# Eight gathers in a row: four U rows then four V rows, in place of U and V in turn

## What is computed

```
eidx = ...                                   # 16 experts per token and head
u = u_tab[eidx]; v = v_tab[eidx]             # rows of 1024 float32
h = gelu(einsum('td,thkd->thk', xk, u))
coef = gate * h
out = einsum('thk,thkd->td', coef, v)
```

## Time and profile before

| | us |
|---|---|
| median of 3 runs | 3058.2 (3057.4 to 3060.53) |
| the profiled execution's own time | 3057.73 |
| its span | 3055.9 |

### The profile page before, as it was taken

How to read it: one execution, slowest core, us unless ns; L and a number is a source line. 1 busy time by engine, 2 the same in 40 slices (tenths; PEclk the granted TensorE clock), 3 DMA queues, 4 the chain that set the end, 5 groups by cost and what they waited for, 6 DMA issues and landing times.

```text
span 3055.9 us, 27644 instructions
## 1 busy us (share of the span) xinstructions
PE 1719.7 (56%) x7829; PEld 779.9 (26%) x7829; DVE 2176.4 (71%) x5291; ACT 917.3 (30%) x3111; POOL 2056.4 (67%) x2169
## 2 busy tenths in 40 slices
PE   8875556777768576666433333355535444335435
PEld 8852223444334233333100000111101111001102
DVE  8787678877776678888766666666677777666553
ACT  2334324333333323322321123333223332123302
POOL 2146667666676776767577777777777777777774
PEclk9987878888889788888665556677757777557668
DMA  6379999999999999999999999999999999999997
GB/s 179 109 270 404 399 400 398 393 391 341 378 386 390 407 404 404 406 398 402 401 401 409 406 405 409 407 407 408 406 409 402 406 409 403 409 401 408 409 409 276
DMA packets 369741, 1165.94 MB, mean 382 GB/s; under 512 B 35433, under 2 KB 95417, under 8 KB 369589
## 3 DMA queue, kind: packets, MB, share of 16 engines
q0 software_dynamic: 304128, 1107.43, 91.9%
q1 hardware_dynamic: 64928, 55.92, 5.7%
q10 hardware_dynamic: 533, 0.83, 0.1%
HBM read 1158.88 MB, written 5.15 MB: 381 GB/s over the span
## 4 chain that ended last, share of the span: by engine, by line
DMA 36%; DVE 25%; POOL 17%; issue 9%; PE 6%; ACT 1%; POOLq 0%; SPq 0%; DVEq 0%; ACTq 0%
DMA ex_u_row<-in_u_tab_dram,ex_eidx 19%; DVE ex_u_row L1991 11%; POOL ex_v_row L1256 9%; POOL ex_u_row L1256 8%; DMA ex_v_row<-in_v_tab_dram,ex_v_idx 8%; DMA ex_u_row<-in_u_tab_dram,m_first_idx 6%; PE ex_acc L1883 3%; DMA ex_u_row<-in_u_tab_dram,ex_few_idx 2%; PE ex_turn L1724 1%; DMA m_wq<-in_w_in_dram 1%; DVE ex_same L1927 1%; DVE ex_same L1929 1%; DVE ex_idx L1930 1%; DVE ex_weight L1985 1%; DVE ex_best_at L1923 1%
## 5 line engine op out<-in xcount | busy, mean ns | idle before, releaser
L1991 DVE CUSTOM_DVE_ANT_0 ex_u_row<-ex_u_row,ex_xn 128x1024 f32<-128x1024 f32 x1056 | 1267.2, 1216 | 717.8 <-DMA ex_u_row<-in_u_tab_dram,ex_eidx 523.5
L1883 PE MATMUL ex_acc<-ex_v_row,ex_weight 128*32 128x512 f32 x4096 | 775.7, 896 | 1168.3 <-DMA ex_v_row<-in_v_tab_dram,ex_v_idx 1158.1
L1256 POOL DMA_INDIRECT ex_v_row<-in_v_tab_dram,ex_v_idx x1024 | 979.7, 957 | 485.7 <-issue 273.5
L1256 POOL DMA_INDIRECT ex_u_row<-in_u_tab_dram,ex_eidx x768 | 737.6, 960 | 242.3 <-issue 176.2
L1883 PEld LDWEIGHTS ex_acc<-ex_v_row,ex_weight 128*32 128x32 f32 x4096 | 155.1, 141 | 1657.7 <-issue 1645.4
L1256 POOL DMA_INDIRECT ex_u_row<-in_u_tab_dram,m_first_idx x256 | 245.7, 960 | 150.3 <-DVEq L2153 72.5
L1483 ACT ACTIVATE ex_hact<-ex_hdot 128x16 f32<-128x16 f32 x66 | 14.3, 216 | 777.7 <-DVE ex_hdot L1991 777.5
L1593 PE MATMUL ex_q<-m_mix,m_wq 128*128 128x384 f32 (+1 forms) x704 | 226.5, 476 | 0.0
L1320 ACT COPY ex_spread_coef<-ex_coef 32x4 f32<-32x4 f32 x1024 | 195.8, 191 | 53.7 <-DVE ex_coef L1976 41.7
L1593 PEld LDWEIGHTS ex_q<-m_mix,m_wq 128*128 128x128 f32 x704 | 135.8, 199 | 103.6 <-issue 42.8
L1309 ACT COPY ex_v_idx<-ex_eidx 32x4 uint32<-32x4 uint32 x768 | 146.0, 190 | 8.3
(11 more groups left out here) (422 smaller groups left out, 2254.7 us busy)
## 6 DMA issues: line engine op xcount, KB each, us to landing
ex_v_row<-in_v_tab_dram,ex_v_idx POOLq DMA_INDIRECT x1024
m_wq<-in_w_q_dram SPq DMA_DIRECT2D x14, 1024.0 KB, 16.5
ex_u_row<-in_u_tab_dram,ex_eidx POOLq DMA_INDIRECT x768, 8.9
fr_w<-in_w_in_dram SPq DMA_DIRECT2D x12, 512.0 KB, 4.7
ex_u_row<-in_u_tab_dram,m_first_idx POOLq DMA_INDIRECT x256, 8.9
m_wq<-in_w_in_dram SPq DMA_DIRECT2D x8, 512.0 KB, 17.8
m_wq<-in_w_out_dram SPq DMA_DIRECT2D x4, 1024.0 KB, 15.6
m_mix<-in_w_ple_gate_dram SPq DMA_DIRECT2D x8, 512.0 KB, 16.7
```

The costliest lines, as they stand in the source:

```text
L1256: pool.indirect_dma_start(out=row[:, :], out_offset=None, in_=table, in_offset=bass.IndirectOffsetOnAxis(ap=pick, axis=0)).then_inc(landed ...
L1883: last = nc.tensor.matmul(acc[g * TS:(g + 1) * TS, half, :], weight[:, b % 2, g * GROUPS + k // PACK, :], v_row[(n - PACK + 1 + g) % V_RIN ...
L1991: nc.vector.tensor_tensor_reduce(out=u_row[n % U_RING][:, :], in0=u_row[n % U_RING][:, :], in1=xn[:, :], scale=1.0, scalar=0.0, op0=ALU.mu ...
```

## The change

POOL's loop skips the V part in three of four steps and issues four V gathers in the fourth. The V gathers are the same, in the same order, with the same waits.

```diff
-                    m = n - V_BEHIND
-                    if 0 <= m < BLOCKS * TOPK:
+                    if n % PACK < PACK - 1:
+                        continue
+                    for m in range(n - PACK + 1 - V_BEHIND, n + 1 - V_BEHIND):
+                        if not 0 <= m < BLOCKS * TOPK:
+                            continue
                         if m % TOPK == 0 and m < PROMPT_BLOCKS * TOPK:
                             pool.wait_ge(v_listed, m // TOPK + 1)
```

## The result

The changed kernel takes 3049.05 us (median of 7 runs, 3045.82 to 3053.19) against 3058.2 us in the same runs, a ratio of 0.9967 (95% interval 0.9956 to 0.9977). That is 9.2 us less. It is faster, as forecast, but by less than half of the 21.2 us.

What follows compares the result with a forecast made beforehand. The prediction took full DMA engines at 409 GB/s as the bound; 18.1 us at the large stalls and 2.6 us at small ones made 20.7 us off 3058.2, so 3037 us, range 3029 to 3061.

Steps and rivals of the forecast that it cites:

- What bounds the kernel, and where time can be won: Whole run: DMA engines are full at 409 GB/s, so order of issue gains only where they run dry.
- The V gate, at 806, 902 and 952 us: POOL's waits for PE's sums there: three more gathers in reserve gain 3.84, 3.84 and 2.7 us.
- The V gate, in the pairs 598/624 and 714/740: Two stalls within 30 us share one reserve, so each pair was counted once, 3.84 us gained.
- the U gate at nothing: POOL's wait for DVE's dots before U gathers: distance stays 16 gathers, 20.5 us, so no cost.
- the sum for the U gate: U slots: 20.5 us less 5.2 us shortest landing leaves 15.3 us; four dots end 7.5 us after the last landing.
- The margin of 8 us: Cover said to remain at the U slots behind DVE's longest ordinary piece, the ranking of a block: about 8 us.
- A queue that is full already costs a load the same whether 7 or 10 gathers stand in it: Mixer weight loads beside gathers: argument against later landing with more gathers queued; no size given.
- the holes only move: Rival: weight loads land later, so the next hole grows; 0 to 4 us given back, 3054 to 3058; chance 0.20.
- A rule weighed against this: DMA queues served in turn: a weight load in a gather hole has the engines alone, lost once filled; 4.7 against 17.8 us.
- The small stretches, 2.6 us: Three small stretches of missing DMA time, 2.0, 1.8 and 1.3 us, not traced to a cause, counted by half.
- Start and end at nothing, 2 us either way: First and last gathers: moved three places but no gain or loss, bounds 2 us either way together.
- Half of it: Rival: stalls at 806, 902 and 952 us chain with earlier ones; 8 to 12 us gained, 3046 to 3050; chance 0.15.

Runs made afterwards that it cites:

- the second trace: The changed kernel profiled and measured once more, nothing altered: 3048.97 us, ratio 0.9967 to the kernel before.
- the form that alternates there: Against the changed kernel, bursts of four only up to step 239, U and V in turn from step 240 on: 3051.63 us, ratio 0.9982.
- The step from four to eight: Against the changed kernel, eight U gathers then eight V gathers in place of four and four: 3094.37 us, ratio 1.0120.
- the table above: Ten rows of weight-load landings: kernel before, changed kernel twice, and variants in burst length, burst steps, sigmoid place or U gathers held to five; 3035.47 to 3111.36 us.

## Why the prediction was off

The time lies in the stated range, in its upper part: 9.2 us were gained of 21.2.

**What bounds the kernel, and where time can be won:** right. The time saved follows the missing time of the DMA engines. From 560 to 1000 us the changed kernel misses 23.3 us in place of 32.4, 9.1 us less, and the median is 9.2 us lower. That the two agree so closely is luck: the second trace misses 19.5 us there, 12.9 us less, with the same median.

**The V gate, at 806, 902 and 952 us:** right in size. Forecast 3.84 us at 806 and 3.84 + 2.7 = 6.5 us at the two others; the windows gave 4.1 and 6.1 us, though 2.7 us of the latter also came in the form that alternates there.

**The V gate, in the pairs 598/624 and 714/740, and the U gate at nothing:** this is the step that failed. Forecast 2 x 3.84 = 7.7 us; the stretch from 560 to 800 us gave -1.1 us, and +2.4 in the second trace. The first half of each pair did pay: 5.9 to 1.2 us missing from 596 to 640 us, and a V wait of 3.21 in place of 8.49 us at 720. Behind it the U gate, priced at nothing, took it back: within 25 us in the first pair, with waits of 6.55 us at 646.89 and 4.4 us more behind it, and with 9.82 us at 737.59 in the second. There a V wait of 7.07 us at 778.00 took the rest. With the cause of DVE's stop taken away, the sigmoid's place on ACT, the same order of gathers misses 5.3 us there in place of 21.1.

Two terms of the sum for the U gate were wrong.

*How long DVE stops.* By the sum, a slot has 15.3 us, and four dots outlast four landings by 5.2 - 3.8 = 1.4 us, so a stop of up to 13.9 us is covered. The prediction saw the wait of 14.65 us over it, and let it go with "the V wait at 747.68 still ends last in it". But the wait is not the whole stop. Before, DVE's last dot ended at 713.58 and the next began here:

```profile
732.01 1.21 DVE L1991 CUSTOM_DVE_ANT_0 ex_u_row<-ex_u_row,ex_xn 128x1024 f32<-128x1024 f32 x1
```

That is 18.4 us, since 3.8 us of mixer work stand between the sigmoid and the dot. In after it was 22.1 us (713.98 to 736.10). And "still ends last" was true of the trace of before alone: once the V wait ahead of it had shrunk, the U wait that ended at 737.59 was the next in line.

*How much the slot covers.* The 15.3 us come from the shortest way from issue to landing, 5.2 us, while the same prediction expected a median of 12.7 us. The measured median is 12.7 us, and it is 14.9 us from 310 to 390 us. The U gather issued at 381.03 us landed after 17.7 us, at 398.7, and POOL wanted its slot again at 405.4 us. That is 6.7 us of cover in place of 15.3, and so a wait of DVE of only 11.50 us, where before had 10.04 us, stopped POOL for 8.81 us at 413.88. The margin of 8 us did not exist where the queue was full. For the ranking of a block it was enough all the same: from 1000 to 2950 us, with the ranking in every block, POOL's longest wait for a dot is 2.0 us. The step from four to eight shows that little was left of it.

**"A queue that is full already costs a load the same whether 7 or 10 gathers stand in it":** this holds in the runs (26.6 us beside gathers of 11.0 and of 14.9 us), but it was no argument against "the holes only move". The queue of before was not full while the loads at 609 us ran. The load there landed 5.8 us later once the hole beside it was filled, the case of the paragraph "A rule weighed against this" rather than that of a deeper queue. Behind it 5.0 us of missing time came up, against the 0 to 4 us that the rival gave back. The rival describes the pairs well and nothing else; at 806 to 970 us the holes were filled and stayed so.

**The small stretches, 2.6 us:** the three, at 490, 1524 and 2722 us, were filled, 2.0, 1.8 and 1.3 us. Others came up: 2.7 us more than before at 410 us, by the U gate, 0.9 us more at 1459 and 2.9 us at 1960 us. By all windows, 240 to 560 us is the same as before and 1000 to 2950 us misses about 1.5 us less (14.9 in place of 16.4). Half of them was counted without a cause; that 1.5 us came out near it is luck.

**Start and end at nothing, 2 us either way:** the tail misses 19.2 us in place of 17.2, at the bound. The claim that "a group of V rows still ends in the same place" held for the order; but POOL, its U gathers done three places earlier, came to a V gather at 2993.66 us 4.26 us too soon, where before had 0.57 us of wait, and those 10 us went from 410 to 323 GB/s. The start, 160 to 230 us, misses 20.4 us in place of 18.8; whether the order does that, no run settled.

**The sum:** 4.1 + 6.1 - 1.1 from 560 to 1000 us, 1.5 behind it, -2.0 in the tail and -1.6 at the start is 7.0 us, against 7.1 us between the spans and 9.2 us between the medians. "Half of it" (3044 to 3052, 0.15) was the case that came true, but not for its reason: the stalls at 806 and behind it were not one chain with the earlier ones.

## What to carry to other kernels

When one issuing engine serves two rings, its order decides how much work each gate has in reserve, and what one gate gains the other must have to spare. Before counting a gain at the gate that stops the engine now, take its wait out of the timeline and look at what stood within some 20 us of it, above all where the other consumer was idle for an unrelated reason. Measure that stop from the last unit of work that frees a slot to the next, and reckon its cover with the landing time of a full queue, not with the shortest. Here, the cheap repair was on an engine that was busy 30% of the time, a sigmoid behind a load-bound block, and it was worth as much as the change itself.

## What was not expected of the hardware

A load of 512 KB on SP's queue does not care how deep the gathers' queue is, only whether it has a hole. Beside gathers that land in a median of 7.2 to 15.2 us, the second load of a pair took 26.0 to 26.8 us in every kernel of the table above; beside a hole of the gathers it took 19.9 to 21.5 us; with no gathers, twelve other loads of 512 KB had a median of 4.7 us. The Trainium skill (DMA: Bandwidth & Descriptors, "Queues, rings and completion order") has each DMA engine go round between the queues that have work. By that a queue with more behind its head costs a load nothing more, and a hole that is filled does cost it; these rows agree with both. For a median over few loads of different kinds, look at the single loads before reading a cause into it.
